# Local attention with the values as stationary operand, inverse softmax sums turned and applied at the eviction, and one projection tile of each item ahead of the turned probabilities

## The reference, cut to what matters

```python
s = jnp.einsum('bnqhgd,bnkhd->bnhgqk', qb, kw) * (1.0 / math.sqrt(HEAD_DIM))
s = jnp.where(mask[None, :, None, None], s, NEG)
m = jnp.maximum(jnp.max(s, axis=-1, keepdims=True), sink_l)
p = jnp.exp(s - m)
denom = jnp.sum(p, axis=-1, keepdims=True) + jnp.exp(sink_l - m)
o = jnp.einsum('bnhgqk,bnkhd->bnqhgd', (p / denom).astype(v.dtype), vw)
...
y_att = rms_norm(windowed_gqa(aq, ak, av, sink), att_g).astype(x.dtype)
...
return jnp.concatenate([y_att, y_ml], axis=-1) @ w_out
...
x = layer_norm(ALPHA * x + y, ln1_g[l], ln1_b[l])
```

## Time and profile before

| | us |
|---|---|
| median of 3 runs | 2225.08 |
| lowest and highest | 2221.23, 2226.53 |
| profiled execution, its own time | 2230.33 |
| its span, first to last instruction | 2228.5 |
| attention stage of the first layer, about | 80 to 282.5 |
| attention stage of the second layer, about | 1158.6 to 1361 |
| mean granted TensorE clock, share of full speed | 0.979 |

### The profile page before, as it was taken

One profiled execution on the slowest core, in us unless ns is written; L12 is line 12 of the kernel. 1 busy time (PEld: TensorE's weight loads), 2 busy tenths in 40 slices (PEclk: granted clock), 3 DMA queues, 4 the chain that ended last, 5 costly groups with the idle time before them and its releaser, 6 DMA issues.

```text
span 2228.5 us, 31496 instructions
## 1 busy us (share of the span) xinstructions
PE 2104.0 (94%) x11392; PEld 1699.3 (76%) x11392; DVE 1331.5 (60%) x2057; ACT 991.3 (44%) x1616; POOL 226.0 (10%) x268
## 2 busy tenths in 40 slices
PE   7989989999999899999798999999999989999997
PEld 7779967888887577777577897778887767777773
DVE  4875487722454765656877647783235476666557
ACT  3554565232422455555245557533333235555552
POOL 0000023000000421001100001300000032100004
PEclk9999999999998999999999999999999999999998
DMA  4154112321102699999511112033120069999995
GB/s 153 57 198 147 39 76 96 105 85 57 57 29 98 252 368 371 386 382 349 189 53 38 39 45 89 20 133 114 57 76 20 32 230 389 375 379 371 377 372 202
DMA packets 78531, 384.85 MB, mean 173 GB/s; under 512 B 10472, under 2 KB 11864, under 8 KB 43608
## 3 DMA queue, kind: packets, MB, share of 16 engines
q1 hardware_dynamic: 55264, 327.31, 38.8%
q0 software_dynamic: 10096, 30.38, 3.9%
q10 hardware_dynamic: 13064, 25.75, 3.1%
HBM read 352.27 MB, written 46.07 MB: 179 GB/s over the span
## 4 chain that ended last, share of the span: by engine, by line
PE 71%; DVE 15%; ACT 8%; issue 3%; DMA 2%; POOL 1%; DVEq 0%; ACTq 0%; POOLq 0%; SPq 0%
PE bank L2197 29%; PE bank L2709 9%; PE bank L2683 8%; PE bank L2673 7%; PE bank L2410 5%; PE bank L2441 2%; ACT scratch L1055 2%; PE bank L2520 2%; DVE scratch L1595 2%; PE bank L2218 1%; DVE weight_slots_parts L1433 1%; PE bank L2649 1%; PE bank L2564 1%; PE bank L2580 1%; DVE small L1601 1%
## 5 line engine op out<-in xcount | busy, mean ns | idle before, releaser
L1903 DVE TENSOR_TENSOR weight_slots_parts<-weight_slots,mixer_region_parts 128x2048 fp32r<-128x2048 f32 x140 | 322.2, 2322 | 84.9 <-ACT mixer_region_parts L1257 84.8
L2197 PE MATMUL bank<-weight_slots_parts,x_transposed_parts 128*128 128x256 f32 (+1 forms) x1248 | 300.3, 335 | 8.6 <-DVE mixed L1555 5.7
L2197 PE MATMUL bank<-x_transposed_parts,weight_slots_parts 128*128 128x512 f32 (+1 forms) x1024 | 265.1, 346 | 8.3 <-DVE mixer_region L1547 5.1
L1257 ACT ACTIVATE mixer_region_parts<-weight_slots 128x2048 fp32r<-128x2048 f32 x140 | 261.1, 1910 | 23.5 <-ACT x_transposed L1332 18.1
L1433 DVE TENSOR_TENSOR weight_slots_parts<-weight_slots,weight_slots_parts 128x2048 fp32r<-128x2048 f32 x58 | 133.0, 2292 | 193.6 <-ACT weight_slots_parts L950 192.8
L2709 PE MATMUL bank<-weight_slots,x_transposed 128*128 128x512 f32 x560 | 247.4, 595 | 0.1
L2197 PEld LDWEIGHTS bank<-weight_slots_parts,x_transposed_parts 128*128 128x128 f32 x1248 | 211.6, 194 | 28.0 <-DVE mixed L1555 6.5
L2683 PE MATMUL bank<-mixer_region_parts,x_transposed_parts 128*128 128x256 f32 x1120 | 207.5, 283 | 1.0 <-DVE weight_slots_parts L1903 0.9
L2197 PEld LDWEIGHTS bank<-x_transposed_parts,weight_slots_parts 128*128 128x128 f32 x1024 | 181.6, 194 | 31.5 <-DVE mixer_region L1547 6.4
L2673 PE MATMUL bank<-mixer_region_parts,x_transposed_parts 128*128 128x512 f32 x560 | 191.8, 414 | 4.6 <-DVE x_transposed_parts L1908 4.6
L2709 PEld LDWEIGHTS bank<-weight_slots,x_transposed 128*128 128x128 f32 x560 | 104.0, 191 | 118.5 <-issue 103.0
(11 more groups left out here) (319 smaller groups left out, 3577.7 us busy)
## 6 DMA issues: line engine op xcount, KB each, us to landing
weight_slots<-in_w_gate SPq DMA_DIRECT2D x70, 1024.0 KB, 7.4
weight_slots<-in_w_up SPq DMA_DIRECT2D x70, 1024.0 KB, 7.1
weight_slots<-in_w_down SPq DMA_DIRECT2D x70, 1024.0 KB, 8.0
weight_slots<-in_w_in SPq DMA_DIRECT2D x20, 1024.0 KB, 5.1
slots_y<-x_transposed ACTq DMA_DIRECT2D x66, 256.0 KB
weight_slots<-in_wkv_mem SPq DMA_DIRECT2D x16, 1024.0 KB, 4.8
slots_y<-in_consts SPq DMA_DIRECT2D x6, 2304.0 KB, 16.8
weight_slots<-in_w_out SPq DMA_DIRECT2D x8, 1024.0 KB, 4.8
```

The source lines that it names most:

```text
L1257: nc.scalar.activation(hi, raw, ACT.Copy).then_inc(moe.high_ready, 1)
L1903: v.tensor_tensor(lo, raw, hi.bitcast(F32), ALU.subtract).then_inc(moe.low_ready, 1)
L2197: ins = pe.matmul(ps, lhs[i](k), rhs[j](k), start=k == 0 and a == 0, stop=k == KD - 1 and a == 2)
```

## The change

It has five parts.

1. The product of probabilities and values is turned round. The values of one key/value head (128 keys by 64) are the stationary operand, and the turned probabilities of two query heads (256 columns) move. A head's output lands in one half of the partitions: 4 or 6 products of 256 columns in place of 8 or 12 of 64. The output then stands turned already, so the 24 transposes (L2218) at the start of the mLSTM stage go.
2. The inverse sums must be turned too. DVE writes the reciprocal of the four sums repeated over 64 columns each (128x256) in place of 128x4; PE turns it in two transposes (`sr`, banks 4 and 5 with the others), ACT copies it out (256 columns, behind the exponentials), and the eviction multiplies the bank by it.
3. In turns 1 to 10 the first stream tile stands ahead of the turned probabilities on PE, and ahead of the masks on DVE. In the same turns ACT handles "ended" ahead of its copies of the turned probabilities, where it stood behind the exponentials. Turns 0, 11 and 12 keep the old order of the tiles.
4. The norm of the attention output is applied later. ACT squares the turned output without a sum, DVE adds four columns each (`sum_squares`, six a layer), PE adds over partitions by products with a column of ones (`rs`), and two pairs of short ACT steps give the factor. It is applied where DVE adds the projection's first half to the residual. The gains go into the weights: the units `wo0` and `wo1` are split in four pieces with a gain each, on ACT and on DVE. The residual's factor moves from the first to the second addition.
5. The high and low parts of the attention output are made from the turned copy in SBUF, not from PSUM.

```diff
+def tile_goes_first(i):
+    return 0 < i < 11
...
 (the loop of PE)
+                        if tile_goes_first(i):
+                            stream_tile(w[0])
                         if i:
                             pe.wait_ge(p_ready, 12 * l + i)
                             turn_probs()
                         if w and i:
-                            stream_tile(w[0])
+                            stream_tile(w[1 if tile_goes_first(i) else 0])
                         if i:
                             if i == 12:
                                 unit_ready("running_max")
                                 spread_maxima(0)
+                            pe.wait_ge(shares_ready, 12 * l + i)
+                            ps = take(("sr", i - 1))
+                            for j in range(2):
+                                ins = pe.transpose(ps[:, j * P:(j + 1) * P], share_rows[:, j * P:(j + 1) * P], ident)
+                            done(ins, ("sr", i - 1))
...
-                            for t in range(GRP):
-                                n, _ = head_at(jp, t)
-                                for k in range(nb):
-                                    ins = pe.matmul(ps[:, t * HD:(t + 1) * HD], ptb[:, (t * nb + k) * P:(t * nb + k + 1) * P],
-                                                    kv[:, k0 + k, NKV * HD + n * HD:NKV * HD + (n + 1) * HD],
+                            for k in range(nb):
+                                for n in range(NKV):
+                                    out = ps[n * HD:(n + 1) * HD, 0:2 * P].rearrange("p (j q) -> p j q", j=2)
+                                    mine = ptb[:, 0:GRP * nb * P].rearrange("p (j n k q) -> p n k j q", j=2, n=NKV, k=nb)[:, n, k, :, :]
+                                    ins = pe.matmul(out, kv[:, k0 + k, NKV * HD + n * HD:NKV * HD + (n + 1) * HD], mine,
                                                     start=(k == 0), stop=(k == nb - 1))
                             done(ins, key)
+                    def sum_tokens(part, c0, n):
+                        key = ("rs", part)
+                        ps = take(key)
+                        for c in range(c0, c0 + n):
+                            pe.wait_ge(att_parts, 12 * l + c + 1)
+                            ins = pe.matmul(ps[:, c - c0:c - c0 + 1], sums_at(c), one, start=True, stop=True)
+                        done(ins, key)
+
+                    sum_tokens(0, 0, NC - 1)
 (the loop of DVE)
-                            step(v.reciprocal(st[:, ro:ro + 4], st[:, ro:ro + 4]))
+                            v.reciprocal(share_rows.rearrange("p (t d) -> p t d", t=GRP),
+                                         st[:, 110:114].unsqueeze(2).broadcast_to([P, GRP, HD])).then_inc(shares_ready, 1)
+                            own(shares_ready)
+                        if tile_goes_first(i):
+                            stream_tile(w[0])
...
+                            tile_drained(dve, ("sr", i - 1))
+                            v.tensor_tensor(y[:, c, 2 * P * jp:2 * P * (jp + 1)], bank_of(key)[:, 0:2 * P], shares, ALU.mult).then_inc(drain_sem(key), 1)
                             tile_drained(dve, key)
-                        for t in w[1:]:
+                        if i >= 8:
+                            sum_squares(i - 8)
+                        for t in w[2 if tile_goes_first(i) else 1:]:
                             stream_tile(t)
 (the loop of ACT)
                         for t in ended:
                             if t[0] == "v":
                                 drain_values(t)
+                            if tile_goes_first(i):
+                                stream_tile(t)
...
+                        if i:
+                            if i > 1:
+                                tile_drained(act, ("pv", i - 2))
+                            drain_copy(("sr", i - 1), shares, 2 * P)
 
                         if 7 <= i < 12:
                             square_of(i - 7)
-                        for t in ended + w[:-1] if i < 12 else ():
+                        for t in (w[:-1] if tile_goes_first(i) else ended + w[:-1]) if i < 12 else ():
 (the splitting of wo0 and wo1, on ACT and on DVE)
+                            for j in range(GRP - 1):
+                                nc.scalar.activation(hi[:, j, :], raw[:, j, :], ACT.Copy, scale=lane_gain[:, j:j + 1])
...
+                            for j in range(GRP):
+                                ins = v.scalar_tensor_tensor(out=lo[:, j, :], in0=raw[:, j, :], scalar=lane_gain[:, j:j + 1], in1=hi[:, j, :],
+                                                             op0=ALU.mult, op1=ALU.subtract)
```

153 lines of the change are left out of this document (99 added, 54 removed).

## The result

| | before | after |
|---|---|---|
| median of the runs, us | 2224.74 | 2297.59 |
| lowest and highest, us | 2221.23, 2226.53 | 2294.76, 2305.08 |
| span of the profiled execution, us | 2228.5 | 2293.2 |
| mean granted TensorE clock | 0.979 | 0.964 |

The changed kernel is slower: the ratio is 1.0335, with a 95% interval of 1.0305 to 1.0364. That is 73 us between the medians and 65 us between the two profiled executions, where 55 were forecast.

The account below looks back on a forecast made before the run. Bound in the convolution stretch: the DVE-ACT chain. 12.2 + 11.8 + 0.7 + 3 = 27.7 us a layer, 55.4 in all: 2285.7 against the profiled execution, 2280 against the median; own range 2262 to 2298, wider range 2240 to 2302.

Parts of the forecast that it names:

- rival D: Clock stays low through turns 6 to 12, 6 us a layer more: 2292 us; chance 0.11.
- Rival B: Repeated input makes the reciprocal as cheap as a plain step, 10.8 us less: 2259 us; chance 0.07.
- rival C: Reciprocal at 8.3 ns a column, 0.45 us more in eight places a layer: 2287 us; chance 0.04.
- The product: Turned product of probabilities and values: saves 0.63 us in 16 items, 1.1 in 8, 19 us of PE in both layers.
- Turns 1 to 5: Convolution turns: waits do not shrink (+2.2 us), 5 reciprocals add 7.9; DVE enters turn 6 10.2 us late.
- Turn 6: Weight unit, masks, exponentials, then the value tile's bank meet here: 12.2 us late at turn 7.
- Value turns: Turns 7 and 8: new 3.4 us wait for ACT to empty the first tile's bank; 18.5 us for 15.4, +3.1 twice.
- Turns 9 to 12: Gate turns: DVE's queue fills; waits of 4 and 2 us on reciprocals; turn 7's scores to last product 95.8 us, +11.8.
- mLSTM start: Two waits on the output's split and 24 transposes go, but ACT sets the end: +0.7 us.
- The clock: Longer idle pieces in turns 3 to 8 and 11 bring the lower clock: 3 us a layer, between 0 and 9.
- Rival A: PE is the bound everywhere and its savings come out, 40 us in all: 2185 us; chance 0.11.
- Rival E: No difference, since weights' loads set the pace of the next stages: 2225 us; chance 0.04.

Follow-up runs that it names:

- e3: Changed kernel with the old tile order in all turns and the reciprocal on 128x4 spread by a DVE copy; 2259.6 us, ratio 1.0147.
- e10: e3 with ACT's first value copy ahead of its sums copy (turns 6 to 8) and DVE's sum of squares behind the turn's tiles; 2246.0 us.
- e2: Changed kernel with the reciprocal on 128x4 again, spread to 128x256 by a DVE copy; 2282.8 us, ratio 1.0232.
- e4: Kernel before the change, with the new tile order alone (product, reciprocal and norm as before); 2259.9 us, ratio 1.0149.
- e12: e4 with ACT copying a turn's first value tile ahead of the transposed probabilities and exponentials; 2244.9 us, ratio 1.0080.
- e1: Changed kernel with the tiles in the old order in all turns; 2280.6 us, ratio 1.0228.
- e8: Kernel before the change, with the first tile ahead in turns 9 and 10 alone; 2233.7 us, ratio 1.0025.
- e6: Changed kernel with ACT copying the first bank of transposed probabilities ahead of the last tile of the turn before (turns 1 to 10); 2310.8 us, ratio 1.0378.

## Why the prediction was right, and where its sizes were off

The direction and the main mechanisms held: new waits through the order of the tiles, and a longer DVE chain through the reciprocal. The time lies within the range of 2240 to 2302, but at the upper end of what the prediction called the forecast's own range (2262 to 2298), and nearer to rival D's 2292 than to 2280. Against the medians it was 18 us too low. 9 of these are in the profiled executions and are followed up here; the rest is that the profiled executions lie above one median and below the other. By its steps:

- **The reciprocal**: 1753 ns, where 1.75 us was taken from the line through the earlier trace rows. Rival B (a plain step) and rival C (2.2 us) fall with that row. The prediction's estimate from the page "VectorE: DVE Perf Modes" of the Trainium skill (its walkthrough of the pipeline: a division repeated 8 times) was 8.3 ns a column; the trace gives 6.8 (1753 / 256), and does not agree.
- **The product**: 8 records take 1.02 us to the next instruction's start and 12 take 1.45, where 1.07 and 1.5 were taken. Column halves run side by side, as the scores' row halves do. With the two transposes (0.31) the gain is 0.37 us in a two-block item. ACT's copy of the sums eats it (e3), and it appears only in e10.
- **Turns 1 to 5**: forecast 10.2 us late at turn 6, of which 2.2 for the order and 7.9 for the reciprocal. Measured +7.7 and +7.9. "5 reciprocals are +7.9" held: taking 1.28 us away in each turn (e2) gives 6.4 and 5.9 us of the 6.4 that it should. "The waits do not shrink: +2.2" was the term too large: DVE's wait for ACT went from 12.3 to 11.6 us and its wait for PE from 4.1 to 2.0, and the order alone (e4) costs 0.7 and 1.1. PE's waits for ACT's copy ahead of the third bank of transposes came, as forecast, in pieces of 5.0 and 3.0 us in the first layer and 3.4 and 2.7 in the second, where 4 to 6 were named. In the sums over turns 0 to 5 the shorter turn 0 hides 1.6 us a layer; that is chance in the clock and no part of the working.
- **Turn 6**: forecast 2 us, measured 7.2 and 6.8. This is the step that failed: "In turn 6 all this meets" counted one wait, for ACT's third copy and the value tile's bank. PE waits four times in a row (1.27, 2.62, 2.62, 1.83). The second of these is for the bank of the product before. DVE evicts it at the end of turn 5, behind that turn's second tile and the finish of its first:

```profile
188.13 0.54 DVE L1607 TENSOR_SCALAR mixer_region<-bank,conv_taps 128x256 f32<-128x256 f32 x1
...
193.39 0.69 DVE L1589 SCALAR_TENSOR_TENSOR mixer_region<-mixer_region,silu_exp 128x512 f32<-128x512 f32 x1 [3.35 <-ACT silu_exp L1047]
194.12 0.42 DVE L1685 TENSOR_TENSOR mixed<-bank,mixer_norm_gains 128x256 f32<-128x256 f32 x1
```

In the old order the eviction stands behind the first tile and the finish of "ended", and the finish of the turn's own first tile comes after it. The new order puts that finish, with its 3.35 us of waiting for ACT, ahead of the eviction, and PE's transposes stand behind both through a bank that the working did not follow. In e4 and e12, without the reciprocal, turn 6 costs 5.0 to 5.8 us more than before, so the order alone is enough for most of it. But it is not needed: e1, with the old order and the reciprocal, has 5.7 and 4.9 us more in turn 6 too, with a wait of 4.2 us for the value tile's bank. Each alone brings 5 us or more, both together 7; only with both undone (e3: 0.6 and 2.4) does it nearly go.
- **Value turns**: forecast 18.5 us with a wait of 3.4. Measured a wait of 3.40, and 20.0 us in turns 7 and 8 of the first layer and 20.0 and 18.6 of the second. In the turn of 18.6 us the two tiles behind the wait of 3.40 took 6.0 us; 1.5 us a turn is the clock.
- **Turns 9 to 12**: forecast waits of 4 and 2 us for the reciprocal, measured 4.31 and 1.62; wo0 took 2.66 us on ACT and 2.74 on DVE, where 2.5 and 2.9 were taken. The last tile of turn 11 waited 0.73 us for its bank, where 3 were forecast. The sum of squares took 1.04, not 0.7. From the scores of turn 7 to the last product the stage takes 100.2 us where 95.8 stood, before the clock.
- **mLSTM start**: forecast +0.7. From the last product to the projection's first it is 12.4 us where 11.3 stood (+1.1), and PE's last wait is for ACT's factor (L1077, 1.02 us), not for the sum of squares (0.67 before that). The next stretch (+4.4 and +3.2) was set at zero to 1: a term put too low. In it PE is busy 87.5 us where it was 84.4, at 0.97 of the clock where it was 1.00; in the second layer 86.1 where it was 84.5, at 0.98. e8, which touches nothing of it, has 1.5 and 1.4 us too, at 0.98 in the first layer, so part of it can come without the new steps. The rest is not explained here.
- **The clock**: forecast 3 us a layer. In the value turns alone it is 3.0 in the first layer and 1.5 in the second. Rival D (2292, low clock through turns 6 to 12) was half right: the clock, 0.95 before in turns 0 to 5 and 1.00 from turn 6 on, is 0.93 in turns 0 to 5, then 0.87, 0.91 and 0.90 in turn 6, turns 7 and 8, and from turn 9 on:

```profile
80.90:185.90 105.00, 88.98 (x502) 70.06 (x500) 86.09 (x140) 52.48 (x110) 0.00 (x0) 0.93 0.40 129
185.90:212.70 26.80, 18.46 (x134) 16.23 (x132) 15.34 (x25) 13.72 (x33) 0.00 (x0) 0.87 0.63 211
212.70:252.80 40.10, 33.30 (x247) 30.75 (x246) 14.65 (x24) 13.74 (x35) 0.00 (x0) 0.91 0.08 27
252.80:325.20 72.40, 60.90 (x411) 50.23 (x410) 43.39 (x78) 46.36 (x104) 2.80 (x8) 0.90 0.24 88
```

In turns 0 to 5 DVE is busy 82% and PE 85%, about as the last part of the prediction asked; from the first scores to the last product it is 232 us, where it named 226 plus the clock as right and 202 as wrong.

- **Rival A** (2185, PE the bound) was to decide if DVE could take 1.6 us more a turn. It could not: e2 gains 6.4 and 5.9 us in turns 1 to 5 from taking 1.28 away in each. Rival E falls with the first table: 35 us a layer are lost in the stage and some 5 come back in the first layer behind it (776.0 to 771.1), where PE's clock is 0.93 before and 0.95 after in one stretch. That return was not forecast.

Summed over both layers: turn 0 -3.2 (no term), turns 1 to 5 +15.6 (20.4 forecast), turn 6 +13.9 (4), turns 7 and 8 +17.2 (12.4, and clock), the rest to the projection +18.1 (12.6, and clock), behind it +7.6 (0 to 2), all else -4.5. The forecast of turns 1 to 5 was 5 us too large, turn 0 gave 3 by chance, and turn 6 was 10 too small; these nearly cancel, so the sum looks better than its parts. Of the 9 us by which it was short, 2 are left of that, 4 lie between turn 7 and the projection beyond the clock's 6, and 7.6 behind it, less the 4.5 that came back elsewhere.

## What to carry to other kernels

When an operation is put ahead on one engine, look for the engine that empties its buffer: with the tile ahead on PE alone, it sat 8.5 us in its bank, because ACT's queue still had it behind the exponentials, and 3.4 us of wait and 1.5 us of lower clock followed. A wait is no measure of what its removal brings: 9.6 us of waits taken away in e6 made the kernel no faster (13 us slower by the medians), since the copy that was moved ahead held up "ended" and, as far as the waits show, the chain behind it. Price a saving on PE together with every small step that it puts on the engines that serve it; 0.37 us of product and 0.38 us of copy left nothing.

## What the runs showed of the hardware

- A reciprocal whose input is four columns repeated 64 times costs as much as one of 256 different columns would by the line of the earlier trace rows: 1753 ns. Reciprocal of the four and a spreading copy cost 179 + 294 ns.
- Products with the stationary operand in two halves of the array's columns ran at the pace of the row halves: 1.02 us for four of 256 columns.
- Behind most idle pieces of PE of 2.6 to 5 us the next products run at the lower of the clock's two levels (1.2 GHz), though not behind each: one wait of 3.40 us in the second layer of after, one of 2.96 in e3 and one of 2.78 in e4 were followed by full speed. Some shorter pieces have it too (1.90 us in turn 10 of the second layer). The price: a tile of 24 records took 4.1 us from start to the next start behind turn 6's waits in after, and 3.0 where nothing waited. In e8 a single piece of 2.78 us, in place of one of 1.27, took the mean clock of 35 us from 1.00 to 0.95. So a wait cost more here than its length.
